# Order of work at the edges of the feed-forwards in a two-part transformer stack on one core: opening unit, last residuals, activation tables, down products

## What is computed

```python
def swiglu(x, w1, w2):
    gu = x @ w1
    return (jax.nn.silu(gu[..., :2816]) * gu[..., 2816:]) @ w2

# first block, each of 2 layers l
x = x + 0.5 * swiglu(rms_norm(x, ffn1_norm[l]), ffn1_w1[l], ffn1_w2[l])
x = x + hybrid_mixer(rms_norm(x, mix_norm[l]), positions, ...)
x = x + 0.5 * swiglu(rms_norm(x, ffn2_norm[l]), ffn2_w1[l], ffn2_w2[l])
# after both
x = rms_norm(x, final_norm)
# second block, each of 2 layers l
mix = hybrid_mixer_2(rms_norm_2(x, attn_pre_norm[l]), cos, sin, ...)
x = x + rms_norm_2(mix, attn_post_norm[l])
h = rms_norm_2(x, ffn_pre_norm[l])
x = x + rms_norm_2(conv_ffn(h, w_up[l], conv_w[l], conv_b[l], w_down[l]), ffn_post_norm[l])
```

## Time and profile before

| | |
|---|---|
| runs | 2298.51, 2305.03, 2306.16 us; median 2305.03 |
| profiled execution | 2305.54 us, of it the span of the profile 2303.8 us |
| mean granted TensorE clock | 0.931 of full speed |
| PE matmul | 2047.1 us busy, 89% of the span |
| PE weight load | 1954.0 us, 85% |
| DVE | 1474.1 us, 64% |
| ACT | 1165.7 us, 51% |
| GpSimd | 152.5 us, 7% |
| loads of weights | 327.27 MB read, 143 GB/s over the span |

### The profile page before, as it was taken

The page is one execution under the profiler, slowest core; times in us unless marked ns, Lnnn a source line. Parts: engine busy times, 40 slices in busy tenths (PEclk is TensorE's granted clock), DMA queues, the critical chain, the costliest instruction groups (busy, mean ns, idle before and its releaser), DMA issues.

```text
span 2303.8 us, 40039 instructions
## 1 busy us (share of the span) xinstructions
PE 2047.1 (89%) x15496; PEld 1954.0 (85%) x15496; DVE 1474.1 (64%) x2084; ACT 1165.7 (51%) x1804; POOL 152.5 (7%) x167
## 2 busy tenths in 40 slices
PE   6999877889999999878889997788799978887998
PEld 6999867889999999877889997675799976667998
DVE  5665698766655656698656656563697465627963
ACT  5445644454444444744554444554575446536753
...
GB/s 207 182 164 190 124 106 97 137 161 201 165 181 183 182 159 173 127 115 98 154 165 185 167 195 137 92 110 19 74 214 153 190 115 110 92 19 110 214 143 118
DMA packets 53535, 329.83 MB, mean 143 GB/s; under 512 B 5936, under 2 KB 6704, under 8 KB 27952
## 3 DMA queue, kind: packets, MB, share of 16 engines
...
HBM read 327.27 MB, written 1.05 MB: 143 GB/s over the span
## 4 chain that ended last, share of the span: by engine, by line
PE 56%; DVE 16%; ACT 11%; DVEq 7%; issue 5%; DMA 4%; POOLq 1%; POOL 1%; ACTq 0%; SPq 0%
PE bank L605 15%; PE bank L606 15%; PE bank L607 15%; DVE w_lo L584 7%; ACT w_hi L578 5%; DMA raw<-in_w 3%; DVEq L915 2%; DVE conv L1243 2%; DVEq L1237 2%; PE bank L617 1%; PE bank L626 1%; PE bank L619 1%; ACT probs L924 1%; PE bank L1542 1%; PE bank L1526 1%
## 5 line engine op out<-in xcount | busy, mean ns | idle before, releaser
L584 DVE TENSOR_TENSOR w_lo<-raw,w_hi 128x2048 fp32r<-128x2048 f32 (+3 forms) x358 | 719.1, 2010 | 425.5 <-ACT w_hi L578 423.3
L605 PE MATMUL bank<-h_hi,w_hi 128*128 128x256 f32 x2704 | 786.1, 291 | 17.2 <-DVE w_lo L584 15.9
L606 PE MATMUL bank<-h_lo,w_hi 128*128 128x256 f32 x2704 | 776.5, 287 | 0.0
L607 PE MATMUL bank<-h_hi,w_lo 128*128 128x256 f32 x2704 | 775.6, 287 | 0.0
L578 ACT ACTIVATE w_hi<-raw 128x2048 fp32r<-128x2048 f32 (+3 forms) x358 | 600.2, 1679 | 172.1 <-DMA raw<-in_w 113.3
L605 PEld LDWEIGHTS bank<-h_hi,w_hi 128*128 128x128 f32 x2704 | 532.3, 197 | 22.9 <-DVE w_lo L584 17.0
L606 PEld LDWEIGHTS bank<-h_lo,w_hi 128*128 128x128 f32 x2704 | 532.1, 197 | 1.0
L607 PEld LDWEIGHTS bank<-h_hi,w_lo 128*128 128x128 f32 x2704 | 530.7, 196 | 0.0
L605 PE MATMUL bank<-hid_hi,w_hi 128*128 128x256 f32 x1056 | 297.1, 281 | 6.5 <-DVE conv L1883 6.5
L606 PE MATMUL bank<-hid_lo,w_hi 128*128 128x256 f32 x1056 | 297.1, 281 | 0.0
L607 PE MATMUL bank<-hid_hi,w_lo 128*128 128x256 f32 x1056 | 297.0, 281 | 0.0
...
## 6 DMA issues: line engine op xcount, KB each, us to landing
raw<-in_w SPq DMA_DIRECT2D x198, 1024.0 KB, 4.8
...
x<-in_x SPq DMA_DIRECT2D x1, 1024.0 KB, 4.8
...
```

Source lines behind the costliest of these rows:

```text
L584: dve.tensor_tensor(w_lo[:, s % SPLIT_SLOTS, 0:n], raw[:, s % RAW_SLOTS, 0:n], w_hi[:, s % SPLIT_SLOTS, 0:n].bitcast(F32), ALU.subtract).t ...
L605: pe.matmul(out, hi, x_hi, start=start, stop=False, skip_group_check=skip)
L606: pe.matmul(out, hi, x_lo, start=False, stop=False, skip_group_check=skip)
L607: return pe.matmul(out, lo, x_hi, start=False, stop=stop, skip_group_check=skip)
```

## The change

- **Opening.** ACT loads the table set LOG_EXP before it waits for anything, makes all 8 high parts of x, splits units 0 and 1, makes the 8 squares, and then splits units 2 and 3. TensorE waits for the high part of unit 0 and the parts of x alone, makes hi·hi and hi·lo of the unit's 16 blocks, waits for the unit's remainder and makes 15 of 16 lo·hi, then the same for unit 1, then the stat, then the two matmuls left.
- **Tails, first block.** Residual 7 comes before the splits of units `base + 14` and `base + 15` on ACT and DVE. Before the second block these two units are split only after the raw parts of its first tiles, and the LOG_EXP set is loaded ahead of residual 7.
- **Tails, second block.** The same: units 14 and 15 are split after the parts of the next layer's x, LOG_EXP is loaded ahead of output 7, and the norms behind it load no table.
- **Sines.** They are taken at the end of the up products of the first and the second feed-forward, where the set SILU is active; no load stands at them there.
- **Second block, early unit.** Unit 4 of the feed-forward is split by ACT in the middle of `true_high` and by DVE behind `true_low`, instead of inside the first gated product.
- **Down products, second block.** They wait for the up product that last used their own bank (18 or 19) instead of the last one (21).

```diff
--- before.py
+++ after.py
@@ -671,9 +671,10 @@
                     last = pe.matmul(bank[:, T + q:T + q + 1], last_sq[:, q * P:(q + 1) * P], ones[:, 0:1], start=False, stop=True)
             last.then_inc(work.done_sem.sem, 1)
 
-        def norm_act_root(act, work, nm, l, n, into, width=T):
-
-            act.preload_act_table_set(LOG_EXP)
+        def norm_act_root(act, work, nm, l, n, into, width=T, loaded=False):
+
+            if not loaded:
+                act.preload_act_table_set(LOG_EXP)
...
@@ -701,9 +702,11 @@
...
-        def true_high(act, nm, l, gain, work, last_raw):
+        def true_high(act, nm, l, gain, work, last_raw, beside=None):
 
             for t in range(KT):
+                if t == KT // 2 and beside is not None:
+                    beside()
                 act.wait_ge(*nm.x_scaled(l, t + 1))
                 act.wait_ge(*(nm.raw_used(l, t + 1) if t < KT - 1 else work.done(l, last_raw)))
                 act.activation(h_hi[:, t], scr[:, t], ACT.Identity, scale=gain(t)).then_inc(nm.true_hi_ready.sem, 1)
@@ -751,8 +754,31 @@
 +            def opening_unit(j):
+
+                s = at + j
+                pe.wait_ge(stream.hi_ready.sem, s + 1)
+                for half in range(2):
+                    for k in range(KT):
+                        if j == 0 and half == 0:
+                            pe.wait_ge(*nm.h_ready(l, KT * m + k + 1))
+                        out, block = banks[j][:, half * T:half * T + T], slice((half * KT + k) * P, (half * KT + k + 1) * P)
+                        for part in (h_hi, h_lo):
+                            pe.matmul(out, w_hi[:, s % SPLIT_SLOTS, block], part[:, k], start=k == 0 and half == 0 and part is h_hi,
+                                      stop=False, skip_group_check=half == 1)
+                weights_ready(pe, s)
+                for half in range(2):
+                    for k in range(KT - half):
+                        opening_remainder(j, half, k)
+
+            def opening_remainder(j, half, k):
+                block = slice((half * KT + k) * P, (half * KT + k + 1) * P)
+                return pe.matmul(banks[j][:, half * T:half * T + T], w_lo[:, (at + j) % SPLIT_SLOTS, block], h_hi[:, k], start=False,
+                                 stop=k == KT - 1, skip_group_check=half == 1)
+
             work.wait_banks_free(pe, l, [(up, j) for j in range(4)])
-            weights_ready(pe, at + 1)
+            if at:
+                weights_ready(pe, at + 1)
             if raw_units:
                 raw_ready = lambda k: nm.h_ready(l, KT * m + k + 1)
                 by_tiles(pe, work, l, [((up, j), at + j) for j in range(2)], raw_ready)
@@ -769,7 +795,14 @@
                     pe.wait_ge(*work.taken(l, (up, j - 4)))
                     up_unit(j, 0)
             else:
-                first_products(pe, nm, work, l, m, [((up, j), at + j) for j in range(2)], lambda: norm_pe(pe, work, nm, l, n))
+                if at:
+                    first_products(pe, nm, work, l, m, [((up, j), at + j) for j in range(2)], lambda: norm_pe(pe, work, nm, l, n))
+                else:
+                    opening_unit(0)
+                    opening_unit(1)
+                    norm_pe(pe, work, nm, l, n)
+                    for j in range(2):
+                        opening_remainder(j, 1, KT - 1).then_inc(work.done_sem.sem, 1)
                 with pe.Fori(0, 5) as it:
                     for u in range(4):
                         pe.wait_ge(*work.taken(l, (up, 0), it * 4 + (2 + u - 4)))
@@ -777,7 +810,7 @@
             with pe.Fori(0, KT // 2) as it:
                 for g in range(2):
                     if work.g.freer[down, 0][0] != "v":
-                        pe.wait_ge(*work.taken(l, (up, FT - 1)))
+                        pe.wait_ge(*work.taken(l, (up, FT - 4 + g)))
                     pe.wait_ge(*work.taken(l, (down, 0), it * 2 + (g - 2)))
                     for half in range(2):
                         s = at + FT + 2 * g + half
@@ -807,6 +840,13 @@
             split.next = at + 16 + FFN_AHEAD
             for j in range(16, FT):
                 gated(j, 0, j % 2, lambda: split.until(at + j + FFN_AHEAD))
+            if l == 0 and w == 0:
+                act.wait_ge(*turned(0, 1))
+                act.activation(trig1[:], trig1[:], ACT.Sin).then_inc(trig_ready.sem, 1)
+            if l == 0 and w == 1:
+                act.wait_ge(*turned2(0, 2))
+                act.activation(cos2[:], cos2[:], ACT.Sin)
+                act.activation(sin2[:], sin2[:], ACT.Sin).then_inc(trig2_ready.sem, 1)
...
@@ -821,10 +861,14 @@
             split.next = base + 12
-            for t in (6, 7):
-                split.until(base + 2 * t)
-                residual(t, 0)
-                split.until(base + 2 * t + 1)
+            split.until(base + 12)
+            residual(6, 0)
+            split.until(base + 13)
+            if l2 == DEPTH:
+                act.preload_act_table_set(LOG_EXP)
+            residual(7, 0)
+            if l2 < DEPTH:
+                split.until(base + 15)
 
         def ffn_dve(dve, l, w, at, n, then, split):
             up, down, work = f"up{w}", f"down{w}", work1
@@ -872,11 +916,14 @@
             split.next = base + 12
-            for t in (6, 7):
-                split.until(base + 2 * t)
-                residual(t, 0)
-                raw_low(dve, n1, l2, n2_, t, gain1(l2, n2_, t))
-                split.until(base + 2 * t + 1)
+            split.until(base + 12)
+            residual(6, 0)
+            raw_low(dve, n1, l2, n2_, 6, gain1(l2, n2_, 6))
+            split.until(base + 13)
+            residual(7, 0)
+            raw_low(dve, n1, l2, n2_, 7, gain1(l2, n2_, 7))
+            if l2 < DEPTH:
+                split.until(base + 15)
@@ -1855,10 +1902,11 @@
             split.next = base + 12
-            for t in (6, 7):
-                split.until(base + 2 * t)
-                output(t, 0)
-                split.until(base + 2 * t + 1)
+            split.until(base + 12)
+            output(6, 0)
+            split.until(base + 13)
+            act.preload_act_table_set(LOG_EXP)
+            output(7, 0)
@@ -1905,7 +1953,7 @@
             split.next = base + 12
-            split.until(base + 15)
+            split.until(base + 13)
@@ -1999,11 +2047,14 @@
         @block.scalar
         def _(act):
             split = Splitter(lambda s: split_hi(act, s), len(ALL_UNITS))
+            act.preload_act_table_set(LOG_EXP)
             act.wait_ge(consts_in.sem, 16)
             act.wait_ge(x_in.sem, 16)
             for t in range(KT):
+                raw_high(act, n1, t, gain1(0, 0, t))
+            split.until(1)
+            for t in range(KT):
                 square(act, n1, 0, t + 1, x[:, t], t % 2)
-                raw_high(act, n1, t, gain1(0, 0, t))
             for l in range(DEPTH):
                 at = LAYER1_AT[l]
                 split.until(at + FFN_AHEAD - 1)
@@ -2012,9 +2063,6 @@
                 ffn_act(act, l, 0, at, (l, 1), split)
                 norm_act_root(act, work1, n1, l, 1, rinv)
                 true_high(act, n1, l, lambda t: gain1(l, 1, t), work1, ("pa", RAW_UNITS1 - 1))
-                if l == 0:
-                    act.wait_ge(*turned(0, 1))
-                    act.activation(trig1[:], trig1[:], ACT.Sin).then_inc(trig_ready.sem, 1)
...
@@ -2022,24 +2070,23 @@
                 ffn_act(act, l, 1, at + FFN1_AT, (l + 1, 0), split)
-            norm_act_root(act, work1, n1, DEPTH, 0, std)
-            act.wait_ge(*turned2(0, 2))
-            act.activation(cos2[:], cos2[:], ACT.Sin)
-            act.activation(sin2[:], sin2[:], ACT.Sin).then_inc(trig2_ready.sem, 1)
+            norm_act_root(act, work1, n1, DEPTH, 0, std, loaded=True)
             for l in range(DEPTH):
                 raw_of_new(act, l, 0)
-                norm_act_root(act, work2, n2, l, 0, rinv, T + 2)
+                split.until(LAYER2_AT[l] + AHEAD)
+                norm_act_root(act, work2, n2, l, 0, rinv, T + 2, loaded=True)
...
                 split.until(LAYER2_AT[l] + FFN2_AT + FFN_AHEAD - 1)
                 norm_act_root(act, work2, n2, l, 2, rinv)
-                true_high(act, n2, l, lambda t: gain2(l, 1, t), work2, ("up0", RAW_UNITS2 - 1))
+                true_high(act, n2, l, lambda t: gain2(l, 1, t), work2, ("up0", RAW_UNITS2 - 1),
+                          lambda: split.until(LAYER2_AT[l] + FFN2_AT + FFN_AHEAD))
                 act.preload_act_table_set(SILU)
                 ffn2_act(act, l, split)
                 act.drain().then_inc(vec2_free.sem, 1)
-                norm_act_root(act, work2, n2, l, 3, std)
+                norm_act_root(act, work2, n2, l, 3, std, loaded=True)
 
         @block.vector
         def _(dve):
@@ -2078,6 +2126,7 @@
                 post_norm_dve(dve, l, 1, lambda t: raw_low(dve, n2, l, 1, t, gain2(l, 1, t)))
                 split.until(LAYER2_AT[l] + FFN2_AT + FFN_AHEAD - 1)
                 true_low(dve, n2, l, lambda t: gain2(l, 1, t))
```

(1 more changed line is left out.)

1 line of the change is left out of this document (added).

## The result

| | before | with the change |
|---|---|---|
| first set of runs, median | 2303.39 us (4 runs) | 2289.56 us (2283.27 to 2292.25, 4 runs) |
| ratio | | 0.9928 (0.9901 to 0.9954) |
| profiled execution | 2305.54, span 2303.8 | 2283.27, span 2281.5 |
| second set | 2308.77 | 2282.28, ratio 0.9881 (0.9851 to 0.9911) |
| third set | 2306.52 | 2277.83, ratio 0.9889 (0.9860 to 0.9918) |

The change is faster by 13.8, 26.5 and 28.7 us in three sets of executions; the two profiled executions first compared differ by 22.3. The ratios and their 95% intervals are estimated over the executions of a set and are not the quotient of its two medians (0.9940 in the first set). One execution of the kernel before in the third set ran in a slower state (3223.58 us, mean granted clock 0.555) and is left out of that ratio. Forecast were 30.0, that is 2275.5 (2266 to 2287).

The account below looks back on a forecast made before the run. TensorE's chain of waits was taken as the bound, with idle stretches at the opening, seams and second block's feed-forward. Terms -8.4 - 2.0 - 3.8 - 5.3 - 9.7 - 2.0 - 1.0 + 2.2 = -30.0 gave 2275.5 us (2266 to 2287).

Parts of the forecast that it names:

- opening, first matmul: Kernel start: TensorE starts at 11.85 instead of 20.25 us, -8.4 us (-9.5 to -6.5).
- first mixer, sines: Layer 0's first mixer: the sine and the table loads it brings go, -2.0 us (-3.2 to -1.0).
- layer 0 to 1: Seam between layers: residual 7 ahead of two remainders cuts the wait by 2.1 and the clock loss by 1.7, -3.8 us.
- first to second block: Seam between blocks: residual 7, Ln and the first high part come earlier, TensorE starts at 1389.2, -5.3 us (-6.9 to -4.5).
- down products: Second block, twice: the 3.26 us wait and 1.7 us clock loss go, -4.85 us each, -9.7 in all.
- end of layer 0, second block: Ln follows the stat without a split and load, -2.45, less 0.45 for late units 14 and 15: -2.0 us.
- unit 4: Second block's feed-forwards: early split moves TensorE's wait to unit 5 without removing it, +1.1 us each, +2.2 in all.
- The stream's debt: Rival, chance 0.03: late units 14 and 15 delay weight loads in following mixers, +12.2 and +17.1 us; with clock fall 2308.
- Unit 4 works as intended: Rival, chance 0.12: second block's TensorE waits at neither unit 4 nor 5, -4.8 us twice instead of +2.2; 2263.7 us.
- The clock falls anyway: Rival, chance 0.15: remaining waits still lower the clock at the layer seam and both down starts, 5.1 us back; 2284.
- Gains are absorbed: Rival, chance 0.09: next waits replace removed ones in the opening, down products and second block's start; half left, 2290 us.
- A load costs twice: Rival, chance 0.04: each of five table loads leaving TensorE's path also held ACT 1.28 us before it, 6.4 more; 2269.1.

Follow-up runs that it names:

- bank wait alone: The kernel before with only the bank-wise wait of the second block's down products; 2297.39 against 2308.77 us, ratio 0.9948.
- sines alone: The kernel before with only the three sines moved to the ends of the first two feed-forwards' up products; 2306.95 against 2312.17 us, ratio 0.9986.
- opening alone: The kernel before with only the new opening; 2300.89 against 2312.17 us, ratio 0.9945.

## Why the prediction was right, and where not

| step | forecast | in the profiles |
|---|---|---|
| opening, first matmul | -8.4 | -8.0 to -8.5 |
| first mixer, sines | -2.0 | -1.8: mean of the column "mixer" 294.0 in the ten profiles without them there (293.1 to 295.2), 295.8 in the three with |
| layer 0 to 1 | -3.8 | -2.08 wait, -1.5 clock |
| first to second block | -5.3 | -5.26, then 0 to +1.4 in the mixer |
| down products | -9.7 | -10.7 or -10.1 (bank wait alone) |
| end of layer 0, second block | -2.0 | -2.48, then +3.9 to +4.8 |
| final norm | -1.0 | -0.97 |
| unit 4 | +2.2 | +2.0 to +2.2 |
| rest of the second block's first mixer | none | -4.7 to -7.6 |

**Right.** The bulk was read off the timelines and came out within 10%. Where a wait was cut short, the clock's fall behind it went too: at the layer seam (2.60 to 0.52 us, clock 1.00) and at both down starts (down stages 64.3 and 63.6 to 62.0). At the layer seam one reading was off without harm: residual 7 had stood behind the remainders of units 13 and 14, and it still stands behind that of unit 13. Unit 4 went as the chain in the earlier trace rows said: the wait moved to unit 5, 3.67 us for 3.7 forecast.

**Wrong: the end of layer 0.** The step "I take 0.45 off since the late units 14 and 15 delay the load chain up to unit 19" named the mechanism and mis-sized it. It put unit 19's landing at 1876.2, that is 29.6 us behind the stage's first product (1849.06 less 2.45), and 0.4 us behind TensorE's release. It was split 34.0 us behind it (1856.85 - 1822.89). Unit 17, released by the remainder that ended at 1838.41, could be split at 1846.43 only, 8.0 us later, where the median load of 1 MB takes 4.8: it was in flight together with unit 16, which was issued 1.3 us before it. Unit 19 took another 6.2 us (1850.66 to 1856.85), with the load of unit 20 behind it from 1852.43. The rival *The stream's debt* had decided at just this place and was given 0.03 at its full price of 29 us (12.2 + 17.1). A partial debt of 4 to 5 us, by far the likelier form, had no case of its own. With unit 14 back in the tail it was gone to the hundredth.

**Missing: the first feed-forward's stream.** The opening was counted in full. In six of the ten profiled executions with the new opening (one of three with the change itself) TensorE came to the mixer 2.1 to 3.0 us ahead of unit 13's remainder, and in five of these the stage behind it took 1.5 us longer (7.3 for 5.8 from its first product to its stat), so that up to 4.5 of the 8.4 are given back. The prediction looked at units 0 to 3 and not at whether all that TensorE needs later moves ahead with it: GpSimd's angles do so less by up to 2 us, and ACT's squares and splits stand behind them. It had GpSimd held by DVE only at the opening's squares, where it cost nothing.

**Missing: the mixers.** "Everything between the seams is TensorE's own row of matmuls, which the change leaves alone" was a reading that the trace of before did not bear out. From the second wait for a feature tile to the next stat of the second block's first mixer TensorE waits 35 us in all, at a granted clock of 0.80. Windows of this stretch, before and sines alone:

```profile
1436.14:1632.75 196.61, 161.62 (x875) 127.79 (x875) 94.52 (x201) 96.16 (x232) 6.19 (x6) 0.80 0.20 70
```

```profile
1441.38:1633.24 191.86, 157.92 (x874) 124.92 (x874) 94.51 (x201) 96.13 (x232) 6.20 (x6) 0.82 0.21 72
```

The three kernels that keep the sines between the blocks (before, bank wait alone, opening alone) take 196.4 to 196.8 us there, sines alone 191.9, and the nine profiles of the change and its variants 189.0 to 191.8. The work is the same (one record more lies on the edge of the first window), and TensorE's waits (33 to 35 us in all of them) account for at most 1.7; the rest of the 4.7 to 7.6 us is clock, 0.795 to 0.804 against 0.812 to 0.832. This is among the largest terms, it repeats (190.1, 190.1 and 189.0 for the change), and no step of the prediction has it. That it goes with the edit of the sines is shown by one profile of sines alone; why the clock stays higher there is open.

**The sum.** With the sizes found: -8.0 + 1.2 (an opening's clock, first down product 6.8 earlier) - 1.8 - 3.6 - 5.3 + 1.0 - 10.7 - 2.5 + 4.8 - 1.0 + 2.0 = -23.9 for the first pair of profiles, and the spans differ by 22.3. That they agree so well is in part luck. The stages that these terms cover differ by -23.3 in this pair and all others by +1.0, but the +1.0 is made of -6.5 in the stretch just told, +3.2 in "its rest", +2.2 in the first block's second mixer, +1.5 in an up stage behind it and +0.7 at a wait of 0.50 us ahead of that mixer. The three medians scatter about the -23.9 by 3 to 10 us.

**Rivals.** *The clock falls anyway* did not happen at the places it named. *Gains are absorbed* happened at a place it did not name, ahead of the first mixer, and not at the three that it did. *A load costs twice* did not: Ln at the final norm gained 0.97 us with its load gone. The Trainium skill (ScalarE: Activation LUTs, What ACT_TABLE_LOAD costs) names a drain of 1.38 us besides; no row here shows it. *Unit 4 works as intended* fell, and the run with the remainder ahead of the taps showed what it would have taken: 132 us in place of 135.2.
